# A mixture-of-experts block after an mLSTM layer: the seam between routing and the first eight experts

## The reference, cut to what matters

```python
h = layer_norm(DEEPNORM_ALPHA * h + mlstm_mixer(h), *ln1)
y = hier_moe(h, ...)
h = layer_norm(DEEPNORM_ALPHA * h + y, *ln2)

# hier_moe
grp_logits = xf @ w_group + b_group            # 4 groups, best one taken
exp_logits = xf @ w_router + b_router          # 8 experts in each, best two taken
hdn = silu(xblk @ w_gate[e]) * (xblk @ w_up[e])    # (128, 1024) @ (1024, 512)
yb = hdn @ w_down[e]                               # (128, 512) @ (512, 1024)
```

## Time and profile before

| | us |
|---|---|
| median of 3 runs (lowest, highest) | 1169.6 (1169.4, 1170.04) |
| the profiled execution | 1168.37 |
| its span | 1166.4 |
| PE busy in it | 1101.9 (94%) |
| DVE busy | 791.7 (68%) |
| ACT busy | 620.2 (53%) |

### The profile page before, as it was taken

How to read it: one execution, slowest core, us unless ns; L and a number is a source line. 1 busy time by engine, 2 the same in 40 slices (tenths; PEclk the granted TensorE clock), 3 DMA queues, 4 the chain that set the end, 5 groups by cost and what they waited for, 6 DMA issues and landing times.

```text
span 1166.4 us, 15483 instructions
## 1 busy us (share of the span) xinstructions
PE 1101.9 (94%) x5339; PEld 898.4 (77%) x5339; DVE 791.7 (68%) x1107; ACT 620.2 (53%) x680; POOL 207.5 (18%) x188
## 2 busy tenths in 40 slices
PE   6999999999999998967999999999999999999983
PEld 5878889678888787856778888888888888888741
DVE  3301233115455787678999989989988989899647
ACT  4311313213334510035878788888888888887632
POOL 3000111100000000002133232332332332322200
PEclk9999999999999999987999999999999999999987
DMA  7523314401211521236999999999999999999764
GB/s 248 180 90 127 110 53 124 130 19 37 71 40 37 199 77 69 73 140 248 420 380 369 382 378 395 393 386 389 381 383 379 384 389 377 392 394 382 278 266 178
DMA packets 65136, 284.10 MB, mean 244 GB/s; under 512 B 16156, under 2 KB 16156, under 8 KB 39620
## 3 DMA queue, kind: packets, MB, share of 16 engines
q1 hardware_dynamic: 52096, 254.14, 57.5%
q0 software_dynamic: 11840, 25.19, 5.9%
q10 hardware_dynamic: 1156, 4.20, 0.9%
HBM read 266.66 MB, written 33.55 MB: 257 GB/s over the span
## 4 chain that ended last, share of the span: by engine, by line
PE 85%; DVE 7%; DMA 3%; DVEq 2%; issue 2%; ACT 1%; SPq 0%; POOLq 0%; ACTq 0%
PE bank L1460 24%; PE bank L1462 24%; PE bank L1461 24%; PE bank L1801 2%; DVE wlo L1331 2%; PE bank L1831 1%; PE bank L1652 1%; PE bank L1654 1%; PE bank L1657 1%; PE bank L1701 1%; PE bank L1612 1%; DMA xt<-hcat 1%; DMA raw_up<-l_w_up 1%; PE bank L1474 1%; PE bank L1666 1%
## 5 line engine op out<-in xcount | busy, mean ns | idle before, releaser
L1460 PE MATMUL bank<-whi,xghi 128*128 128x512 f32 x512 | 203.2, 397 | 1.6 <-DVE xglo L1340 1.4
L1462 PE MATMUL bank<-whi,xglo 128*128 128x512 f32 x512 | 200.8, 392 | 0.0
L1461 PE MATMUL bank<-wlo,xghi 128*128 128x512 f32 x512 | 200.4, 391 | 0.0
L1331 DVE TENSOR_TENSOR wlo<-raw_down,whi 128x2048 fp32r<-128x2048 f32 x64 | 146.3, 2292 | 34.6 <-ACT whi L776 34.6
L1460 PE MATMUL bank<-whi,xhi 128*128 128x512 f32 (+1 forms) x400 | 163.7, 409 | 2.9 <-ACT vext L695 1.6
L1462 PE MATMUL bank<-whi,xlo 128*128 128x512 f32 (+1 forms) x400 | 158.2, 395 | 0.0
L1461 PE MATMUL bank<-wlo,xhi 128*128 128x512 f32 (+1 forms) x400 | 158.1, 395 | 0.0
L1331 DVE TENSOR_TENSOR wlo<-raw,whi 128x2048 fp32r<-128x2048 f32 x64 | 146.0, 2287 | 2.9 <-ACT whi L776 1.5
L1331 DVE TENSOR_TENSOR wlo<-raw_up,whi 128x2048 fp32r<-128x2048 f32 x64 | 146.1, 2284 | 2.0 <-ACT whi L776 2.0
L776 ACT ACTIVATE whi<-raw_up 128x2048 fp32r<-128x2048 f32 x64 | 122.4, 1914 | 32.5 <-PE bank L1462 24.0
L776 ACT ACTIVATE whi<-raw_down 128x2048 fp32r<-128x2048 f32 x64 | 122.5, 1914 | 28.1 <-PE bank L1462 22.9
(11 more groups left out here) (308 smaller groups left out, 1627.2 us busy)
## 6 DMA issues: line engine op xcount, KB each, us to landing
raw<-l_w_gate SPq DMA_DIRECT2D x64, 1024.0 KB, 8.5
raw_up<-l_w_up SPq DMA_DIRECT2D x64, 1024.0 KB, 8.5
raw_down<-l_w_down SPq DMA_DIRECT2D x64, 1024.0 KB, 8.9
raw<-l_w_in SPq DMA_DIRECT2D x5, 2048.0 KB, 10.3
yy<-expert_rows SPq DMA_DIRECT2D x7, 1024.0 KB, 13.0
xt<-hcat SPq DMA_DIRECT2D x8, 512.0 KB, 3.5
o_rows<-stage POOLq DMA_DIRECT2D x16, 256.0 KB, 2.6
qkT<-qk_rows SPq DMA_DIRECT2D x16, 256.0 KB, 3.7
```

Source lines behind the costliest of these rows:

```text
L1331: tt(wlo[k][:, halves(p)], raw_e[k][:, halves(p)], whi[k][:, halves(p)].bitcast(F32), ALU.subtract).then_inc(e_lo[k], 1)
L1460: t.matmul(out, lh, rh, start=first, stop=False)
L1461: t.matmul(out, lh, rl, start=False, stop=False)
L1462: return t.matmul(out, ll, rh, start=False, stop=last)
```

## The change

- SP loads the first half of down(0) straight after up(0), the second half after the first gather has landed. Then it loads, with experts 1 to 5 fixed and without the list, for j from 1 to 4: up(j), down(j), gate(j+1). The loop with up, gate, down starts at j = 5.
- PE and DVE have items 0 to 7 written out and wait for `routed_n` after them; ACT waits for it after item 1; POOL has eight fixed items.
- `item_count` is cut in two (`item_count`, `item_list`). The list's work follows DVE's items 0 (count), 1 (list, which signals `routed_n`), 2 (`past_128`), 3 (`past_128_items`), 4 and 5 (`past_128_slots` by halves). `list_past_128` moves to PE's item 6, `rows_past_128` to DVE's item 7.
- For the last tile: the statistics of the first half are taken before the second half exists; inverse root before the subtraction; the choices (up to `r_a`) before the shift; `r_acum` is written after the slots, with a new semaphore `counted`.
- Gate(0) starts when half of the gathered rows is split (`first_gate`), and DVE splits the rows before the second half of up(0); ACT splits them before the second half of down(0).
- POOL waits for `routed` behind the stores, and some temporaries have other addresses.

```diff
         sp.wait_ge(N["y_mm"], 2 * NT)
         load_expert(0, 0, 1)
+        load_expert(0, 0, 2, [0])
         for s in range(2):
             sp.wait_ge(h1_stored[s], 16 * (NT // 2))
-        load_expert(0, 0, 2)
         sp.wait_ge(gathered[0], 16)
+        load_expert(0, 0, 2, [1])
         load_expert(1, 1, 0)
+        for j in range(1, 5):
+            load_expert(j, j, 1)
+            load_expert(j, j, 2)
+            load_expert(j + 1, j + 1, 0)
         sp.wait_ge(N["routed_n"], 1)
...
-        with sp.Fori(0, pairs_m1) as i:
+        with sp.Fori(2, pairs_m1) as i:
...
# POOL
+                if j == 0:
+                    pool.wait_ge(N["routed"], 1)
...
-        for j in range(6):
+        for j in range(8):
             scatter(j, j % 2)
             gather(4 + j, j % 2)
...
# ACT
-        for k in (1, 2):
-            for p in range(2):
-                hi_expert(0, k, p)
+        for p in range(2):
+            hi_expert(0, 1, p)
+        hi_expert(0, 2, 0)
         xg_hi(0, 0)
+        hi_expert(0, 2, 1)
         hi_expert(1, 0, 0)
         xg_hi(1, 1)
         hi_expert(1, 0, 1)
         silu(0)
-        act.wait_ge(N["routed_n"], 1)
...
         item(0, 0)
         item(1, 1)
+        act.wait_ge(N["routed_n"], 1)
...
# DVE
+        residual(NT - 1, 0)
+        top_two(NT - 2)
+        half_sums(NT - 1, 0)
+        slots(NT - 2)
+        residual(NT - 1, 1)
+        half_sums(NT - 1, 1)
+        row_sums(NT - 1)
+        inverse(NT - 1)
+        centre(NT - 1)
+        choice(NT - 1)
+        shift(NT - 1)
+        marks(NT - 1)
...
         slots(NT - 1)
+        so_far(NT - 1)
+        dve.drain()
+        dve.sem_inc(N["counted"], 1)
...
-        for k in range(2):
-            for p in range(2):
-                lo_expert(0, k, p)
+        for p in range(2):
+            lo_expert(0, 0, p)
+        lo_expert(0, 1, 0)
         xg_lo(0, 0)
+        lo_expert(0, 1, 1)
         for p in range(2):
             lo_expert(0, 2, p)
-        item_count()
         lo_expert(1, 0, 0)
...
-            if isinstance(j, int) and j < 3:
-                (past_128, past_128_items, past_128_slots)[j]()
+            if isinstance(j, int):
+                if j == 0:
+                    item_count()
+                if j == 1:
+                    item_list()
+                if j == 2:
+                    past_128()
+                if j == 3:
+                    past_128_items()
+                if j in (4, 5):
+                    past_128_slots(j - 4)
...
# PE
+        def first_gate():
+            for q in range(2):
+                pe.wait_ge(N["xg_lo"], q + 1)
+                up_or_gate(0, 0, 0, 2, N["g_mm"], range(4 * q, 4 * q + 4))
...
-            if isinstance(j, int) and j == 3:
+            if isinstance(j, int) and j == 6:
                 list_past_128()
```

More of the change, by code:

```diff
@@ L245, in build @@
     cursor[0] = offsets["qsT"]
+    r_cmp = at("r_cmp", [1, EXTRA, NE])
+    r_cnt = at("r_cnt", [P, NE])
+    r_ex8 = at("r_ex8", [P, NE, 8])
+    r_e = at("r_e", [1, 3, ITEMS])
+    assert cursor[0] <= offsets["r_kn"]
+    cursor[0] = offsets["qsT"]
     r_ohrx = at("r_ohrx", [P, NT, 2, P], BF16)
@@ L250, in build @@
     assert cursor[0] <= offsets["r_kn"]
[L252 to L257, removed]
     hh = [over(("raw1", "whi0")[n // 4], f"hh{n}", [P, 4, D])[:, n % 4, :] for n in range(NT)]
@@ L307, in build @@
         u_mm c_done rs_done nn_done gated_done ot_mm o_hi o_lo y_mm z_done h1_done ht_mm ht_cp lg_mm lg_done
-        cc_mm cc_cp cc_out cc_in wg_scaled r_hot rk_mm r_slot list_mm cnt_mm routed routed_n
+        cc_mm cc_cp cc_out cc_in wg_scaled r_hot rk_mm r_slot list_mm counted cnt_mm routed routed_n
         rx_done rx_mm routed_x w_arg w_exp pool_passed
@@ L398, in load_residual, with load_expert @@
             sp.dma_start(hres[i % 2][:], hcat[tile_cols(i), :]).then_inc(res_landed[i % 2], 16)
-        def load_expert(j, e, k):
+        def load_expert(j, e, k, parts=range(2)):
             src = (gate_w, up_w, down_w)[k]
-            for p in range(2):
+            for p in parts:
                 wait(sp, e_lo[k], j * 2 + (p - 1))
@@ L574, in scatter @@
                                  bounds_check=last_row, oob_is_err=False).then_inc(scattered[b], 16)
-        pool.wait_ge(N["routed"], 1)
         for s in range(2):
@@ L588, in _ @@
         pairs_m2 = pool.value_load(npm1[0:1, 2:3], min_val=NE // 2 - 2, max_val=ITEMS // 2 - 2)
-        with pool.Fori(3, pairs_m2) as i:
+        with pool.Fori(4, pairs_m2) as i:
             for b in range(2):
@@ L856, in _ @@
         item(1, 1)
+        act.wait_ge(N["routed_n"], 1)
+        pairs_m1 = act.value_load(npm1[0:1, 0:1], min_val=NE // 2 - 1, max_val=ITEMS // 2 - 1)
         with act.Fori(1, pairs_m1) as i:
@@ L1110, in residual, with half_sums, row_sums, centre @@
             stt(z1[i % 2][:, s], hres[i % 2][:, s], ALPHA, ps[Z_BANK[(2 * i + q) % 4]][:], ALU.mult, ALU.add).then_inc(N["z_done"], 1)
-        def norm_sums(i):
+        def half_sums(i, q):
             dve.drain()
-            z, b = z1[i % 2], i % 2
-            for q in range(2):
-                v.bn_stats(lst[:, q, :], z[:, q * 512:(q + 1) * 512])
+            v.bn_stats(lst[:, q, :], z1[i % 2][:, q * 512:(q + 1) * 512])
+        def row_sums(i):
             dve.drain()
-            v.bn_aggr(lmv[:, b, 0:2], lst[:].rearrange("p a b -> p (a b)"))
+            v.bn_aggr(lmv[:, i % 2, 0:2], lst[:].rearrange("p a b -> p (a b)"))
             dve.drain()
+        def centre(i):
+            b = i % 2
             if i == 0:
@@ L1123, in norm_sums, with inverse, shift, norm_rows @@
             wait(dve, h1_stored[b], 16 * (i // 2))
-            stt(h1t[b][:], z[:], lmv[:, b, 0:1], g1[:], ALU.subtract, ALU.mult)
-        def norm_rows(i):
+            stt(h1t[b][:], z1[b][:], lmv[:, b, 0:1], g1[:], ALU.subtract, ALU.mult)
+        def norm_sums(i):
+            half_sums(i, 0)
+            half_sums(i, 1)
+            row_sums(i)
+            centre(i)
+        def inverse(i):
             b = i % 2
             rsqrt_column(lmv[:, b, 2:3], lmv[:, b, 1:2], lmv[:, b, 3:4])
+        def shift(i):
+            b = i % 2
             stt(h1t[b][:], h1t[b][:], lmv[:, b, 2:3], b1[:], ALU.mult, ALU.add).then_inc(N["h1_done"], 1)
+        def norm_rows(i):
+            inverse(i)
+            shift(i)
         iota_g = r_iota[:, 0:GROUPS]
@@ L1145, in logit_terms, with choice @@
             dve.drain()
-        def top_two(i):
+        def choice(i):
             b, row = i % 2, lg[:, i, :]
@@ L1169, in top_two, with marks @@
             tt(r_a[:, i, :], r_oh[:, i, 0, :], r_oh[:, i, 1, :], ALU.add).then_inc(N["r_hot"], 1)
+        def marks(i):
+            b = i % 2
             wait(dve, N["list_mm"], i - 1)
@@ L1172, in top_two, with so_far @@
             ts(r_rhs[b][:, 1], r_oh[:, i], float(2 * P * i), None, ALU.mult)
+        def so_far(i):
             dve.drain()
             tt(r_acum[:, i + 1, :], r_acum[:, i, :], r_a[:, i, :], ALU.add)
+        def top_two(i):
+            choice(i)
+            marks(i)
+            so_far(i)
         def slots(i):
@@ L1205, in item_count, with item_list @@
             tt(r_ex[:, 2, :], r_ex[:, 1, :], r_ex[:, 0, :], ALU.subtract)
+        def item_list():
             tt(r_cmp[:], r_iota[0:1, 0:EXTRA].unsqueeze(2).to_broadcast([1, EXTRA, NE]), r_ex[0:1, 1, :].unsqueeze(1).to_broadcast([1, EXTRA, NE]), ALU.is_ge)
@@ L1241, in past_128_items, with past_128_slots @@
             tt(r_rhsx[1], r_eq[:], r_val1[:].unsqueeze(2).unsqueeze(3).to_broadcast([P, NT, 2, EXTRA]), ALU.mult)
-        def past_128_slots():
+        def past_128_slots(half):
             slot = r_kn[:, 2].rearrange("p n k -> p (n k)")
-            tt(r_ohrx[:].rearrange("p n k s -> p (n k) s"), r_iota[:].unsqueeze(1).to_broadcast([P, 2 * NT, P]), slot.unsqueeze(2).to_broadcast([P, 2 * NT, P]), ALU.is_equal).then_inc(N["rx_done"], 1)
+            m = slice(half * NT, half * NT + NT)
+            tt(r_ohrx[:].rearrange("p n k s -> p (n k) s")[:, m, :], r_iota[:].unsqueeze(1).to_broadcast([P, NT, P]), slot[:, m].unsqueeze(2).to_broadcast([P, NT, P]), ALU.is_equal).then_inc(N["rx_done"], 1)
         def rows_past_128():
@@ L1319, in _ @@
         norm_rows(3)
-        for i in range(4, NT):
+        for i in range(4, NT - 1):
             residual(i, 0)
@@ L1326, in _ @@
             norm_rows(i)
-        top_two(NT - 1)
+        residual(NT - 1, 0)
[10 more added lines that the diff above has]
+        marks(NT - 1)
         def lo_expert(j, k, p):
@@ L1360, in _ @@
         lo_expert(1, 0, 1)
-        dve.wait_ge(N["routed_n"], 1)
-        pairs_m1 = dve.value_load(npm1[0:1, 0:1], min_val=NE // 2 - 1, max_val=ITEMS // 2 - 1)
         def item(j, b, ahead=2):
@@ L1371, in item @@
                 weight_diagonals(j)
-            if isinstance(j, int) and j == 3:
+            if isinstance(j, int) and j == 7:
                 rows_past_128()
@@ L1382, in item @@
                 lo_expert(j + 1, 2, 1)
```

(23 more changed lines are left out.)

1 line of the change is left out of this document (removed).

## The result

| | before | after |
|---|---|---|
| median of the timed runs, us (lowest, highest; runs) | 1169.82 (1169.4, 1171.25; 4) | 1188.01 (1185.73, 1188.38; 4) |
| the profiled execution | 1168.37 | 1188.38 |
| its span | 1166.4 | 1186.6 |

The ratio is 1.015, with an interval of 1.0136 to 1.0163. The change costs 18 us, where 8.5 was forecast: sign and mechanism are right, and the time lies above the range.

A forecast was written before the change was run, and what follows sets the result against it. PE was taken as the bound, DVE and transfers close behind. Seam −2.5, item 0 −1.6 and three items of 21.6 us put item 5 +7.6 late; list matmuls +0.95 made +8.5: 1178 as a median, range 1169 to 1182.

The forecast's parts named there:

- T5: Start of PE's transposes of item 5's hidden rows; forecast at 651.5 against 643.95, +7.6 us.
- Rivals 1, 2 and 3: Load order harmless, 1168, chance 0.13; plainly faster, 1165, chance 0.10; half the harm, 1174.5, chance 0.17.
- Z: Start of the last tile's transposes of z, just before the seam; a counting point set with the result, not forecast.
- A + 11.3: Landing of gate's first half after SP issues the next down; with 10.3 more, items of 21.6 us, not 17.75.
- My bounds, 10.2 to 12.4: Gate's landing after down's issue, without POOL's traffic or with both transfers; over three items the sum is +5.2 to +11.8.
- T0 − Z: Seam up to item 0's hidden-row transposes on PE; their start forecast at 548.5 instead of 551.05, −2.5 us.
- T1 − T0: Time between hidden-row transposes of items 0 and 1 on PE; the latter forecast at 568.7 against 570.33, −1.6 us.
- T5 = T4 + 17.75: From item 4's to item 5's hidden-row transposes: a settled item, since gate(6) is loaded ahead of down(5).
- Rival 4: PE's clock also falls in the waits of items 1 to 3, only the last loss staying: +12.5, 1182, chance 0.10.
- The list's 0.95: The list's matmuls on PE, moved into item 6, behind the start of item 5's hidden-row transposes: +0.95 us.
- ACT's wait for `routed_n`: After item 1 on ACT; claimed to be covered by the late gate, costing about 1.1 us without that cover.
- the list and the store meet at 523: In the seam: token list ready at 522.9, ACT's store of the h1 row landing at 523.0.

The follow-up runs named there:

- e10: The changed kernel with POOL's gathers of items 4 to 7 fetching 16 rows instead of 128; 1184.23 us.
- e7: The changed kernel with 24 unused float32 products put on PE before the hidden-row transposes of items 0 to 3; 1184.97 us.
- e3: e1 with ACT's items 0 to 7 written out and its wait for `routed_n` after them; 1166.05 us.
- e1: The changed kernel with SP loading gate(j+1) ahead of down(j) for experts 1 to 4; 1166.1 us.
- e12: e3 with the last tile's shift put ahead of the choices again; 1166.82 us.
- e2: The kernel before, with SP's loop loading down(j) ahead of gate(j+1) for all experts; 1331.34 us.
- e5: e1 with both halves of down(0) loaded straight after up(0); 1169.42 us.

## Why the prediction was right in its direction and wrong in its size

**The mechanism held, as argued.** SP issued down(j+1) ahead of gate(j+2), ACT waited for the gates of experts 3, 4 and 5, PE waited for `gu`, and from item 5 on an item took 17.75 again (T6 − T5 is 17.76). Rivals 1, 2 and 3 fall with T5 at 664.67, which is Z + 148.8 where before has Z + 132.0.

**The step that failed: "That lands at A + 5.2 (the queue has run empty), its second half 2.5 later, gate another 2.5, with one of scatter and gather between, 1.1: A + 11.3."** A, SP's issue of the next down, was 570.85, 594.05 and 617.27, and the gates were taken up at 583.89, 607.18 and 630.33: A + 13.04, 13.13, 13.06. The cycle was 23.2, not 21.6. The remainder, 10.2 forecast as 10.3, was right. The landings of the first such group, one row each (issue to landing):

```profile
raw_down<-l_w_down SPq DMA_DIRECT2D x1, 1024.0 KB, 5.6
```
```profile
raw_down<-l_w_down SPq DMA_DIRECT2D x1, 1024.0 KB, 8.0
```
```profile
raw<-l_w_gate SPq DMA_DIRECT2D x1, 1024.0 KB, 10.4
```

The first half lands at 576.4. The second is issued 2.2 us after the first, since DVE frees it only then, and lands at 581.1, 4.65 us behind it; gate comes 2.7 later. The 2.5 of a settled queue was used where the queue was just filling, and POOL's scatter (issued 569.71, landed 9.0 later) and gather (issued 572.02, 10.6) both fell into the same stretch, where I let in one. Of the 1.75 us of excess the gather explains 0.4 to 0.6 (e10) and the first half 0.4 (5.6, not 5.2). The other 0.75 to 0.95 I would lay on the scatter and on the wait for the second half; no run took the scatter away, so that stays open. My bounds, 10.2 to 12.4, were the same few rows in other sums, which is why they missed. Three items: 1.6 + 1.4 + 1.8 = 4.8 us.

Beside it, on the Trainium skill: the prediction set the fit for GpSimd's path ("DMA: Bandwidth & Descriptors", "Anatomy of one DMA — SWDGE (gpsimd) path"; an estimate of 4.4 us for a half) against the row of SP's queue, 5.2. The changed kernel's half in an empty SP queue took 5.6, with a scatter beside it, further from that estimate.

**The first items: 2.6 us.** T0 − Z was 37.32; forecast were 2.5 us saved and 1.8 came. Landings were forecast 2.5 us apart from the first, but down(0)'s second half, beside the gathers of items 1 and 2, took 7.5 us from its issue at about 533.3, where 5.2 was taken. So gate(2) was used at Z + 44.8, not Z + 41.7, and T1 − T0 was 22.19, not 20.25. This is the same mistake as above. The 0.7 of T0 is not safe: PE waited 1.31 us before gate(1)'s first chunks,

```profile
551.05 0.47 PE L1518 MATMUL bank<-whi,xghi 128*128 128x512 f32 x1 [1.31 <-issue]
```

until just after ACT's silu(0), which comes behind the high parts of gate(1), had ended at 550.95 (that this is what it waited for is read from the order, not tested); e10, the same up to here, waited 0.23 and has T0 − Z 36.17.

**T5 = T4 + 17.75: 1.7 us.** The clock fell at 645 and PE worked at half speed until 649, some 3.5 us, and at 1.00 from there on. Rival 4 named this mechanism as a thing that might stand beside my forecast: its place was right (only the loss behind T4 counts, shown by e7), its size (4 us) too large. PE had been idle 3.92 us just before it fell, about what rival 4 named.

Together 0.7 + 1.9 + 4.8 + 1.7 is 9.1, with the forecast's 8.5 that makes 17.6, as the table's rows from T0 − Z to T5 − T4 (16.7) and the list's 0.95 do; the medians differ by 18.2. The list's 0.95 lies in the table's last row, which even so is 0.5 shorter; no cause was looked for in the 1.5 us.

**What was hidden was rightly called hidden.** ACT's wait for `routed_n` shows 5.74 us in the changed kernel and costs nothing there: T3 − T2, 22.67, is shorter than both its neighbours. Without the late gate it costs 1.6 us (e3 against e1), forecast 1.1. The list's matmuls, +0.95, came as said.

**In the seam one reason was wrong.** I let the list and the store meet at 523. The list was ready 526.65 + 0.18 = 526.83, and the gather started later, on the store's landing (timeline of POOL, after):

```profile
528.33 1.65 POOL L569 DMA_INDIRECT xg<-h_rows,tokrow  x1 [312.48 <-DMA h_rows<-h1t]
```

The store's landing, 3.1 us after its issue where 2.6 were taken, sets the gather; nothing is to be won by taking the choices out of the row's way either (e12), since the store then meets down(0)'s first half.

## What to carry to other kernels

Where each kind of operand has one buffer and one queue issues in order, the order of the loads has to be the order in which the buffers are *used*, and also that in which they come free: one load that waits for its buffer holds every load behind it, and a head start of 15 us was used up within the first item here (T1 − T0 was already 22.19). A landing time taken from a settled queue (spacing 2.5 us) isn't that of a queue that was empty (5.6 for the first, 4.65 more for the second, 2.2 of it a later issue): price a stall by rows in which the queue was just filling, and let all other queues' transfers of that moment in. And value parts of a change together as well as alone: seam and list gave nothing apart (1.0006 and 1.0007) and 0.34% together, because, by one profile of each, each alone ran into what the other takes away: the seam into the list's wait, the list into rows as late as before.

The best version is the changed kernel with the two lines swapped (e1, 1166.1 us; with ACT's late wait e3, 1166.05), 0.3 to 0.4% faster than the kernel before.

## What the runs showed of the hardware that was not expected

- The clock can fall in one run and not in the next at the same step. In before's profile PE was idle 1.96 and 2.14 us between 454 and 466 and the clock stayed at 1.00; in e2, whose kernel is the same up to there, 1.97 us of idleness at the first of these places were followed by four microseconds at 0.50, and in the changed kernel 2.15 us were.
- Products that nobody reads, 22 us of them, laid ahead of PE's waits make a kernel 3 us faster (e7). From Z to T5 its profile shows 2.1 of these, 1.6 of them behind the last wait, where the clock stays at 1.00.
- A store of half a megabyte lands after 2.6 us with no load beside it, after 3.1 with the last 1 us of a load, and after 5.2 (e5) and 5.7 (e12) with some 4 to 5 us of loads.
- A half-speed PE costs nothing as long as its work fills a wait that would have come: T4 − Z is 129.3 with a mean clock of 0.91 between T0 and T4, and 128.8 with 1.00 there (e7).
